# Sums of squares in the attention heads: exact fp32 products replaced by a rounded square and its remainder, and one temporary moved

## The chip, the cores and the metric

One Trainium2 chip, one of its cores. The metric is the device time of one execution in microseconds (us), lower is better. The kernel is a single launch. Its engines work from separate instruction streams and meet at semaphores: TensorE (PE, with its weight loads as PEld), VectorE (DVE), ScalarE (ACT), GpSimd (POOL) and SyncE (SP).

## What is computed

Two blocks run one after the other on a sequence of 1024 tokens with 1024 channels. The second has two layers over 1040 tokens (16 meta tokens in front, padded to 1044 columns here). The change is in its attention, 8 heads of 96 dimensions in each layer. The rest (pooling, gates, projections, the whole first block) is untouched. The part that matters:

```python
def rmsnorm_2(x, gain):
    xf = x.astype(jnp.float32)
    inv = lax.rsqrt(jnp.mean(xf * xf, axis=-1, keepdims=True) + NORM_EPS)
    return (xf * inv * gain.astype(jnp.float32)).astype(x.dtype)

def mla(...):
    q = (c_q @ w_q_b).reshape(B, L, N_HEADS, QK_HEAD_DIM)
    kv = (c_kv @ w_kv_b).reshape(B, L, N_HEADS, QK_NOPE_DIM + V_HEAD_DIM)
    k_nope, v = kv[..., :QK_NOPE_DIM], kv[..., QK_NOPE_DIM:]
    k_pe = jnp.broadcast_to(k_rope_raw[:, :, None, :], (B, L, N_HEADS, QK_ROPE_DIM))
    k = jnp.concatenate([k_nope, k_pe], axis=-1)
    q = rmsnorm_2(q, g_qn)
    k = rmsnorm_2(k, g_kn)
    # rotation of the last 32 dimensions of q and k, then causal softmax attention
```

So every head needs, for each token, the sum of 96 squares of its query and the sum of 96 squares of its key. Tokens lie along the free dimension and the 96 dimensions along partitions, so the sum runs over partitions and is made by TensorE: a product with a matrix of ones (`ones96`, with zeros in the 32 rows that hold the rolled copy for the rotation) leaves the sum in every row of a PSUM bank.

## The kernel before

**Precision.** Products that need fp32 accuracy are made of values split in two: `hi` is the value rounded to the fp32r type, `lo` the remainder, and hi*hi, hi*lo and lo*hi are added up in PSUM. The two sums of squares are the exception: `key_sum` (L985) and `query_sum` (L995) multiply plain fp32 squares by plain fp32 ones in one matmul instruction each. The profile shows such an instruction as two matmul records and two weight loads.

**A head.** For head g the 1044 columns are cut into three waves: two of 384 columns and one of 276. A wave goes: `key_value_part` (L957) leaves raw keys and values in the bank `acc_n`; ACT (`key_value_evict`, L1638 and two copies) squares the keys and moves keys and values out; `query_part` (L973, three parts of six matmuls) leaves raw queries in `acc_q`; ACT (`query_squares`, L1654) squares them. `key_sum` then fills `acc_n` again, ACT (`key_scale`, L1664 Ln and L1667 Exp) makes the inverse root, `turn_values` (L1006) transposes the values into the same `acc_n`, ACT copies them out (`values_in`, L1202), `query_sum` fills `acc_n` a third time and ACT (`query_scale`, L1675 and L1678) makes the queries' inverse root. Each user of `acc_n` waits for the reader before it. DVE applies the rotation to the queries (`query_table`, L2342 to L2344), scales and splits the keys (`key_norm`, L2364 to L2368) and the queries (`query_norm`, L2352 to L2356), and reduces rough scores to row maxima (`maximum`, L2377).

**The order of work** is written out by hand, with no planner. Every engine runs `for h in range(-1, MH)` and in it 15 steps `n`. In a pass h, PE makes the scores, the exponents' products with the values and the later rough scores of head h, and between them the waves of head g = h + 1, with wave 0 at n = 0 to 4, wave 1 at n = 5 to 9 and wave 2 at n = 10 to 14. The pass h = -1 has no scores: it only prepares head 0. The last pass prepares nothing. There are thus 16 heads prepared in all, 14 of them inside a pass that also has scores and 2 (one for each layer) in an opening pass. `key_sum` stands at n = 2, 7, 12, `turn_values` at n = 3, 8, 13 and `query_sum` at n = 4, 9, 14. PE's first matmul that needs a normalized wave is `rough_scores` (L1022): at n = 7 for wave 0 (it waits for `q_hi` and `k_hi`), at n = 12 for wave 1, at n = 2 of the next pass for wave 2.

DVE's stream is in order, and `do` makes it wait for the completion of each of its instructions. Its order in a pass is: n=0 `key_norm` of wave 2, n=1 `query_norm` of wave 2, n=2 two maxima, n=3 maximum, `head_out` (L2394, L2395) of the pass before, maximum, n=4 `query_table` of wave 0 and two maxima, n=5 a maximum, `maxima_of`, `key_norm` of wave 0, n=6 `head_out`, `query_norm` of wave 0, n=7 and n=8 a maximum each, n=9 maximum, `query_table` of wave 1, n=10 `key_norm`, n=11 `query_norm` of wave 1, n=12 two maxima, n=13 two maxima and `head_out`, n=14 maximum, `maxima_of`, `query_table` of wave 2. In the pass h = -1 DVE also makes constants at n = 6 and n = 8.

**Ahead of the heads** DVE splits eight chunks of the latent activations (L2326, by the helper at L1818 and L1819), each when PE has released the chunk. `ones96` is a slice of the constants; its rows for the rotated part of the keys find their squares in `X[:, 6, :]` (L1607, once for each layer).

**Memory.** The rotation's temporary `rope_tmp` (L214) lies in the work buffer `R_` behind the row maxima. `G_` is an fp32r view of rows 8 to 15 of that buffer.

**POOL** splits the streamed weights, one unit of 1024 columns for each head in this stage, and no part of it is in the change. SP only issues the loads of weights.

Of the kernel before, what the change touches and what calls it, by code (L numbers as in the profile page):

```python
# [7 lines left out]
F32 = mybir.dt.float32  # L8
F32R = mybir.dt.float32r
I32 = mybir.dt.int32  # L10
ALU = mybir.AluOpType
# [4 lines left out]
P = 128  # L16
# [132 lines left out]
def build(nc, xT, metaT, pos, params, consts, bands, lru_w, wstream, outT):  # L149
    with ExitStack() as ctx:  # L150
# [59 lines left out]
        ident_r, causal_r, after_r = (G_[:, idr0 + P * i:idr0 + P * i + P] for i in range(3))  # L210
        row_max = G_[:, idr0 + 3 * P:idr0 + 3 * P + 34 * TB]
        extra0 = idr0 + 3 * P + 34 * TB
        assert extra0 + QP <= 8 * RW
        rope_tmp = R_[:, 8 * RW + extra0:8 * RW + extra0 + QP]  # L214
        head_inv = tuple(R[:, 18, QP * i:QP * i + QP] for i in range(2))
        qb = tuple(X_[:, 4 * TP + QP * i:4 * TP + QP * i + QP] for i in range(2))
        qsq = tuple(X_[:, 4 * TP + QP * i:4 * TP + QP * i + QP] for i in (2, 3))
# [78 lines left out]
        for name in tuple(f"x_in{j}" for j in range(KC)) + tuple(f"reload{j}" for j in range(KC)) + (  # L296
            "consts_in", "meta_in", "lru_in", "bands_in", "xre_in",
            "w_in0", "w_in1", "w_hi_done", "w_lo_done", "unit_done",
            "ready0", "ready1", "free0", "free1",
            "aux_ready0", "aux_ready1", "aux_free0", "aux_free1",  # L300
            "a_ready", "a_used",
            "f_ready",
            "sq_ready", "sq_free", "sum_ready", "rs_ready", "x_squared", "x_paired",
            "dve_step", "act_step",
            "to_dve", "to_act", "to_pe",
            "act_to_pe",
            "spilled", "m_spilled", "g_spilled", "g_spilled_late", "stored", "pos_in", "t_spilled", "t_in",
            "kv_raw", "q_raw", "k_free", "q_free", "k_squared", "q_squared", "k_sum", "q_sum", "kn_free", "qn_free",
            "rs_k", "rs_q", "k_normed", "q_normed", "k_hi", "q_hi", "k_lo", "q_lo",
            "v_turned", "v_in",  # L310
            "rough_ready", "rough_max", "max_ready", "max_turned", "max_row",
            "s_ready", "p_in",
            "piece_done", "piece_free", "piece_squared", "piece_total", "piece_summed", "piece_scale",
            "piece_y", "piece_hi", "piece_lo",
            "lru_done", "conv_done", "conv_summed", "conv_centred", "conv_squared", "conv_variance", "conv_rs",
            "conv_normed", "gate0", "gate1", "gate_log", "conv_gate", "vt_ready", "vt_copied", "sc_ready", "sc_free", "sc_max", "sc_exp", "mx_ready", "max_taken",
            "pt_ready", "pt_copied", "av_ready", "av_copied", "sum_taken", "weights_due", "weights_ready",
            "gain_squared", "gain_root", "meta_squared", "meta_summed", "meta_scale", "weighed", "plain",
            "weighed_free", "plain_free", "x1_squared", "x1_total", "x1_summed", "x1_scale", "x1_done",
            "pv_done", "pv_ready0", "pv_ready1", "inv_ready", "inv_used", "av_free0", "av_free1",  # L320
        ):
            sems[name] = sem(name)
# [129 lines left out]
        def _(pe):  # L452
# [435 lines left out]
            for l in range(LAYERS):  # L888
# [90 lines left out]
                def key_sum(g, pc):  # L979

                    k = wave(l, g, pc)
                    c0, w = QP * pc, piece_width(pc)
                    pe.wait_ge(*n_free[0])
                    pe.wait_ge(sems["k_squared"], k)
                    nc.tensor.matmul(acc_n[:, 0:w], ones96, X[:, 6, c0:c0 + w], start=True,  # L985
                                     stop=True).then_inc(sems["k_sum"], 1)
                    n_free[0] = (sems["kn_free"], k)

                def query_sum(g, pc):

                    k = wave(l, g, pc)
                    w = piece_width(pc)
                    pe.wait_ge(*n_free[0])
                    pe.wait_ge(sems["q_squared"], k)
                    nc.tensor.matmul(acc_n[:, 0:w], ones96, qsq[k % 2][:, 0:w], start=True,  # L995
                                     stop=True).then_inc(sems["q_sum"], 1)
                    n_free[0] = (sems["qn_free"], k)

                def turn_values(g, pc):
# [98 lines left out]
                for h in range(-1, MH):  # L1098
                    g = h + 1
                    more = g < MH  # L1100
                    for n in range(NB):
# [6 lines left out]
                        if more:  # L1108
                            if n in (7, 8, 9):
                                rough_scores(g, n - 7, 0)  # L1110
                            if n == 12:
                                rough_scores(g, 3, 0)
                            if n == 13:
                                rough_scores(g, 4, 1)
                            if n == 14:
                                rough_scores(g, 5, 1)
                            if n in (0, 5, 10):
                                key_value_part(g, n // 5)
                            if n % 5 in (1, 2, 3):
                                query_part(g, n // 5, n % 5 - 1)  # L1120
                            if n in (2, 7, 12):
                                key_sum(g, n // 5)
                            if n in (3, 8, 13):
                                turn_values(g, n // 5)
                            if n in (4, 9, 14):
                                query_sum(g, n // 5)
                            if n == 10:
                                turn_maxima(g, 0)
                            if n in (12, 13):
                                rough_scores(g, n - 8, 0)  # L1130
# [43 lines left out]
        def _(act):  # L1174
# [364 lines left out]
            for l in range(LAYERS):  # L1539
# [93 lines left out]
                def key_value_evict(g, pc):  # L1633
# [1 line left out]
                    k = wave(l, g, pc)  # L1635
                    c0, w = QP * pc, piece_width(pc)
                    act.wait_ge(sems["kv_raw"], k)
                    do(nc.scalar.activation(X[top, 6, c0:c0 + w], acc_n[top, 0:w], ACT.Square), "k_squared")  # L1638
                    if k > 2:
                        act.wait_ge(sems["k_lo"], k - 2)  # L1640
                    do(copy(kb[k % 2][top, 0:w], acc_n[top, 0:w], param(f"kn_{l}", 0, top)))
# [2 lines left out]
                def query_squares(g, pc):  # L1644
# [6 lines left out]
                        await_unit(0)  # L1651
                    if k > 2:
                        act.wait_ge(sems["q_normed"], k - 2)
                    do(nc.scalar.activation(qsq[k % 2][:, 0:w], acc_q[:, 0:w], ACT.Square), "q_squared")  # L1654

                def key_scale(g, pc):

# [126 lines left out]
        def _(dve):  # L1784
# [423 lines left out]
            for l in range(LAYERS):  # L2208
# [110 lines left out]
                for j in (6, 7, 0, 1, 2, 3, 4, 5):  # L2319
# [3 lines left out]
                    else:  # L2323
                        c["a_used"].step()
                        dve.wait_ge(sems["a_used"], c["a_used"].value())
                    split(R[:, 8 + j, wide], Ah[:, j, :], Al[:, j, :], "a_ready")  # L2326
                await_free(0)
                await_free(1)
                do(vec.tensor_copy(S_[:, 40:41], S_[:, 60:61]), "to_act")
                top = slice(64, 128)  # L2330

                def query_table(g, pc):
# [1 line left out]
                    k = wave(l, g, pc)  # L2334
                    c0, w = QP * pc, piece_width(pc)
                    q = qb[k % 2]
                    if pc == NQP - 1:
                        unit.step()
                    dve.wait_ge(sems["q_squared"], k)
                    if k > 2:  # L2340
                        dve.wait_ge(sems["q_lo"], k - 2)
                    do(vec.tensor_tensor(q[:, 0:w], acc_q[:, 0:w], R[:, 17, c0:c0 + w], ALU.mult), "q_free")  # L2342
                    do(vec.tensor_copy(rope_tmp[rope, 0:w], q[ROPE:2 * ROPE, 0:w]))
                    do(vec.tensor_tensor(q[rope, 0:w], q[rope, 0:w], rope_tmp[rope, 0:w], ALU.add))  # L2344

                def query_norm(g, pc):

# [66 lines left out]
                for h in range(-1, MH):  # L2414
# [4 lines left out]
                    for n in range(NB):  # L2419
                        if h >= 0:  # L2420
                            if n == 0:
                                key_norm(h, 2)
                            if n == 1:
                                query_norm(h, 2)
                        if more and n == 4:
                            query_table(g, 0)
                        if h >= 0:
# [221 lines left out]
```

## Time and profile before

| what | value |
|---|---|
| median of 3 runs | 3119.41 us (3118.04 to 3122.75) |
| the profiled execution, its own time | 3116.02 us |
| its span | 3113.5 us (2.5 us of its time lie outside the span) |
| mean granted TensorE clock | 0.991 |
| PE busy | 2999.5 us, 96% of the span |
| DVE busy | 1426.5 us, 46% |
| ACT busy | 738.6 us, 24% |
| POOL busy | 1109.3 us, 36% |
| chain that ended last, PE's share | 89%; DVE 8%; ACT 2% |

The page gives busy shares of the whole span. The chain that ended last follows each instruction back to what released it, and lists the pieces with their start and length; in it a matmul stands with the time by which it moved the end of the matmuls on, while the timeline shows each matmul from its own start to its own end, and these overlap. "issue" in the chain is time in which the engine waited for nothing that the profile could name. The heads of the two layers are at about 1688 to 2012 us and 2644 to 2967 us, and their passes repeat every 38.8 us.

### The profile page before, as it was taken

How to read it: one execution, taken by the hardware profiler on the slowest of the kernel's cores; microseconds unless marked ns; L12 is line 12 of the kernel's file. 1: busy time of each engine (PE TensorE's matmuls, PEld its weight loads, DVE VectorE, ACT ScalarE, POOL GpSimd, SP SyncE). 2: the span in 40 equal slices, each digit the busy share in tenths (PEclk: the TensorE clock that was granted, in tenths of full speed). 3: DMA queues.
4: the chain of work that ended last, by engine and by line, in shares of the span. 5: the costliest groups of instructions: out<-in, count | busy, mean ns of one | idle time of the engine just before them, and what ended most of it. 6: DMA issues, size and time to landing. Idle time of an engine off the chain costs nothing.

```text
span 3113.5 us, 41248 instructions
## 1 busy us (share of the span) xinstructions
PE 2999.5 (96%) x16332; PEld 2672.7 (86%) x16332; DVE 1426.5 (46%) x1781; ACT 738.6 (24%) x1285; POOL 1109.3 (36%) x1335
## 2 busy tenths in 40 slices
PE   7999889999999999899999999999999999899999
PEld 5777667888888888899998888899999999788899
DVE  3796754332222349500114666656520022666761
ACT  3144421000000023001112555402100111555500
POOL 3652144444444445433433111143533433111132
PEclk9999999999999999999999999999999999999999
DMA  2111111111111111212112000241312112000142
GB/s 112 48 34 38 70 52 42 48 47 47 47 47 47 47 48 69 76 44 101 48 62 75 15 15 14 79 142 41 112 53 96 48 49 89 27 15 15 38 169 81
DMA packets 47444, 182.60 MB, mean 59 GB/s; under 512 B 6080, under 2 KB 6208, under 8 KB 46912
## 3 DMA queue, kind: packets, MB, share of 16 engines
q1 hardware_dynamic: 31248, 113.19, 10.9%
q10 hardware_dynamic: 16048, 67.28, 5.7%
q8 instruction: 113, 1.85, 0.2%
q14 instruction: 35, 0.29, 0.0%
HBM read 150.06 MB, written 30.39 MB: 58 GB/s over the span
## 4 chain that ended last, share of the span: by engine, by line
PE 89%; DVE 8%; ACT 2%; issue 1%; DMA 0%; POOL 0%; ACTq 0%; DVEq 0%; POOLq 0%
PE acc L476 66%; PE acc L973 4%; PE aux L1089 4%; PE acc L1068 4%; PE acc L581 3%; PE acc L1022 2%; PE acc L957 1%; PE acc L985 1%; PE acc L995 1%; DVE act_lo L1851 1%; DVE work L1858 1%; DVE act_lo L1819 1%; PE acc L1006 0%; DVE work L2232 0%; DVE residual L2248 0%
## 5 line engine op out<-in xcount | busy, mean ns | idle before, releaser
L404 POOL TENSOR_TENSOR w_lo<-w_raw,w_hi 128x256 fp32r<-128x256 f32 (+1 forms) x924 | 849.0, 949 | 17.2
L476 PE MATMUL acc<-act_hi,w_hi 128*128 128x348 f32 (+1 forms) x2896 | 709.6, 345 | 31.0 <-DVE work L2257 8.3
L476 PE MATMUL acc<-act_lo,w_hi 128*128 128x348 f32 (+1 forms) x2896 | 707.9, 344 | 0.0
L476 PEld LDWEIGHTS acc<-act_hi,w_hi 128*128 128x128 f32 x2896 | 506.0, 189 | 76.0 <-issue 30.3
L476 PE MATMUL acc<-act_hi,w_lo 128*128 128x348 f32 (+1 forms) x2896 | 562.1, 344 | 0.0
L476 PEld LDWEIGHTS acc<-act_lo,w_hi 128*128 128x128 f32 x2896 | 507.6, 189 | 39.3
L424 POOL TENSOR_TENSOR small<-shape_consts 128x1 f32<-128x1 f32 x192 | 45.4, 236 | 1367.1 <-PE acc L476 1257.4
L476 PEld LDWEIGHTS acc<-act_hi,w_lo 128*128 128x128 f32 x2896 | 490.5, 188 | 39.4
L476 PE MATMUL acc<-ff_split,w_hi 128*128 128x512 f32 (+1 forms) x1376 | 314.0, 375 | 3.2 <-DVE ff_split L1819 3.2
L476 PEld LDWEIGHTS acc<-ff_split,w_hi 128*128 128x128 f32 x1376 | 246.9, 188 | 50.1 <-DVE ff_split L1819 4.3
L2107 DVE TENSOR_TENSOR residual<-acc,residual 128x1024 f32<-128x1024 f32 (+1 forms) x82 | 100.7, 1228 | 383.1 <-PE acc L476 383.0
L413 POOL CAST w_hi<-w_raw 128x1024 fp32r<-128x1024 f32 x23 | 25.6, 1115 | 596.3 <-PE acc L973 510.1
L1068 PE MATMUL acc<-ff_split 128*128 128x276 f32 (+5 forms) x864 | 208.6, 354 | 0.1
L425 POOL CAST w_hi<-w_raw 128x1024 fp32r<-128x1024 f32 x192 | 201.5, 1050 | 0.0
L1089 PE MATMUL aux<-work 128*128 128x276 f32 (+5 forms) x576 | 175.4, 400 | 0.0
L1483 ACT ACTIVATE work<-acc 128x1024 f32<-128x1024 f32 x32 | 32.7, 1026 | 574.3 <-PE acc L476 568.0
L1068 PEld LDWEIGHTS acc<-ff_split 128*128 128x128 f32 x864 | 140.8, 190 | 31.3 <-issue 0.7
L476 PE MATMUL acc<-ff_split,w_lo 128*128 128x512 f32 (+1 forms) x688 | 166.6, 373 | 0.0
L1707 ACT ACTIVATE work<-acc 128x384 f32<-128x384 f32 (+2 forms) x240 | 104.4, 435 | 200.5 <-PE acc L1068 149.8
L2156 DVE TENSOR_TENSOR work<-work 128x1024 f32<-128x1024 f32 x32 | 40.7, 1273 | 239.9 <-ACT work L1483 239.8
L1202 ACT ACTIVATE work<-acc 64x384 f32<-64x384 f32 (+5 forms) x153 | 93.4, 620 | 217.4 <-PE acc L476 177.2
L476 PEld LDWEIGHTS acc<-ff_split,w_lo 128*128 128x128 f32 x688 | 124.2, 188 | 22.0
(296 smaller groups left out, 3765.0 us busy)
## 6 DMA issues: line engine op xcount, KB each, us to landing
w_raw<-in_wstream SPq DMA_DIRECT2D x215, 512.0 KB, 3.2
spill_m<-residual ACTq DMA_DIRECT2D x2, 4176.0 KB, 13.1
spill_g<-work ACTq DMA_DIRECT2D x16, 522.0 KB, 2.7
residual<-spill_m ACTq DMA_DIRECT2D x16, 522.0 KB, 5.9
work<-spill_g ACTq DMA_DIRECT2D x16, 522.0 KB, 8.2
residual<-spill_x ACTq DMA_DIRECT2D x16, 522.0 KB, 4.1
spill_x<-residual ACTq DMA_DIRECT2D x8, 522.0 KB, 4.5
spill_x<-residual ACTq DMA_DIRECT2D x1, 4176.0 KB, 11.6
```

Of the source, the lines that this page charges most:

```text
L404: ins = nc.gpsimd.tensor_tensor(Wl[:, s, c0:c0 + w], Wraw[:, s, c0:c0 + w], Wh[:, s, c0:c0 + w].bitcast(F32), ALU.subtract)
L424: nc.gpsimd.tensor_tensor(S_[:, 62:63], C_[:, 128:129], C_[:, 128:129], ALU.add)
L425: nc.gpsimd.tensor_copy(Wh[:, s, :], Wraw[:, s, :]).then_inc(sems["w_hi_done"], 1)
L476: ins = nc.tensor.matmul(acc[0:m, s, p, 0:w], wt[:, ws, w0 + j * m:w0 + j * m + m], x[:, k, p * w:p * w + w], start=(first and t == 0), st ...
L581: ins = nc.tensor.matmul(acc[:, s, p, 0:w], wt[:, ws, k * P:k * P + P], x[:, k, p * w:p * w + w], start=(first and t == 0), stop=(end and ...
L973: ins = nc.tensor.matmul(acc_q[:, 0:w], wt[:, w_head[0], j * P:j * P + P], x[:, j, c0:c0 + w], start=(j == 0 and t == 0), stop=(j == 5 and ...
L1022: ins = nc.tensor.matmul(acc_r[bank][:, 0:n], qh[:, min(P * i, LASTQ):min(P * i, LASTQ) + P], kh[:, 512 * p:512 * p + n], start=True, stop ...
L1068: ins = nc.tensor.matmul(out, k2[kt][:, c0:c0 + P], q2[qt][:, lo:lo + w], start=m == 0, stop=(m == 2 and not diag))
L1089: ins = nc.tensor.matmul(aux[:, b % 2, lo - QP * pc:lo - QP * pc + w], values(h)[:, t, :], prob(k)[:, at:at + w], start=t == 0, stop=end)
L1202: return nc.scalar.activation(out, in_, ACT.Copy, scale=scale)
L1707: do(nc.scalar.activation(prob(k)[:, 0:w], src, ACT.Exp), "p_in")
L2107: do(vec.tensor_tensor(x, acc_view(s, pieces), x, ALU.add), f"free{s}")
```

## The change

Four things, all in the attention stage:

- The squares are kept twice. ACT squares each wave a second time, with output in the fp32r type (`k_sq[0]`, `q_sq[0]`), beside the fp32 squares. DVE then subtracts the rounded square from the exact one (`key_square_low` at n = 1, 6, 11 and `query_square_low` at n = 4, 9, 14, both ahead of the other work of their step), which gives `k_sq[1]` and `q_sq[1]`. The rows of the rotated keys are split once for each layer after chunk 7 of the eight chunks.
- `key_sum` and `query_sum` are two fp32r matmuls each (high part, then remainder) against `ones96_r`, an fp32r copy of the ones that DVE makes once for each layer. They wait for the remainder, not for the square.
- In the pass h = -1, `key_sum` goes to n = 3, 8, 13, right ahead of `turn_values`; in the other passes it stays.
- `rope_tmp` moves from the work buffer into chunk 6 of the residual buffer. `query_table` no longer waits for `q_squared`; that wait is in `query_square_low`.

```diff
-        rope_tmp = R_[:, 8 * RW + extra0:8 * RW + extra0 + QP]
+        q_sq = tuple(G_[:, extra0 + QP * i:extra0 + QP * i + QP] for i in range(2))
+        ones96_r = G_[:, extra0 + 2 * QP:extra0 + 2 * QP + P]
+        k_sq = tuple(G_[:, 6 * RW + TP * i:6 * RW + TP * i + TP] for i in range(2))
+        rope_tmp = X_[:, 6 * TP + QP:6 * TP + 2 * QP]
...
 def key_sum(g, pc):
-                    pe.wait_ge(sems["k_squared"], k)
-                    nc.tensor.matmul(acc_n[:, 0:w], ones96, X[:, 6, c0:c0 + w], start=True,
-                                     stop=True).then_inc(sems["k_sum"], 1)
+                    pe.wait_ge(sems["k_square_low"], k)
+                    for i in range(2):
+                        ins = nc.tensor.matmul(acc_n[:, 0:w], ones96_r, k_sq[i][:, c0:c0 + w], start=(i == 0), stop=(i == 1))
+                    ins.then_inc(sems["k_sum"], 1)
...
 def query_sum(g, pc):
-                    pe.wait_ge(sems["q_squared"], k)
-                    nc.tensor.matmul(acc_n[:, 0:w], ones96, qsq[k % 2][:, 0:w], start=True,
-                                     stop=True).then_inc(sems["q_sum"], 1)
+                    pe.wait_ge(sems["q_square_low"], k)
+                    for i in range(2):
+                        ins = nc.tensor.matmul(acc_n[:, 0:w], ones96_r, q_sq[i][:, 0:w], start=(i == 0), stop=(i == 1))
+                    ins.then_inc(sems["q_sum"], 1)
...
-                            if n in (2, 7, 12):
+                            if n in ((3, 8, 13) if h < 0 else (2, 7, 12)):
                                 key_sum(g, n // 5)
...
 def key_value_evict(g, pc):
-                    do(nc.scalar.activation(X[top, 6, c0:c0 + w], acc_n[top, 0:w], ACT.Square), "k_squared")
+                    if k > 1:
+                        act.wait_ge(sems["k_square_low"], k - 1)
+                    nc.scalar.activation(X[top, 6, 0:w], acc_n[top, 0:w], ACT.Square)
+                    do(nc.scalar.activation(k_sq[0][top, c0:c0 + w], acc_n[top, 0:w], ACT.Square), "k_squared")
...
 def query_squares(g, pc):
-                    do(nc.scalar.activation(qsq[k % 2][:, 0:w], acc_q[:, 0:w], ACT.Square), "q_squared")
+                    nc.scalar.activation(qsq[k % 2][:, 0:w], acc_q[:, 0:w], ACT.Square)
+                    do(nc.scalar.activation(q_sq[0][:, 0:w], acc_q[:, 0:w], ACT.Square), "q_squared")
...
                     split(R[:, 8 + j, wide], Ah[:, j, :], Al[:, j, :], "a_ready")
+                    if j == 7:
+                        split(X[rr, 6, :], k_sq[0][rr, :], k_sq[1][rr, :], "dve_step")
                 await_free(0)
                 await_free(1)
+                do(vec.tensor_copy(ones96_r, ones96))
...
 def query_table(g, pc):
-                    if pc == NQP - 1:
-                        unit.step()
-                    dve.wait_ge(sems["q_squared"], k)
...
+                def key_square_low(g, pc):
+                    dve.wait_ge(sems["k_squared"], k)
+                    do(vec.tensor_tensor(k_sq[1][top, own], X[top, 6, 0:w], k_sq[0][top, own].bitcast(F32),
+                                         ALU.subtract), "k_square_low")
+
+                def query_square_low(g, pc):
+                    if pc == NQP - 1:
+                        unit.step()
+                    dve.wait_ge(sems["q_squared"], k)
+                    do(vec.tensor_tensor(q_sq[1][:, 0:w], qsq[k % 2][:, 0:w], q_sq[0][:, 0:w].bitcast(F32),
+                                         ALU.subtract), "q_square_low")
...
+                        if more and n in (1, 6, 11):
+                            key_square_low(g, n // 5)
+                        if more and n in (4, 9, 14):
+                            query_square_low(g, n // 5)
                         if more and n == 4:
                             query_table(g, 0)
```

## Rows read from the trace of the kernel before

**Rows 1.** The page's first part: busy time, share of the span, instructions of each engine.

```profile
PE 2999.5 (96%) x16332; PEld 2672.7 (86%) x16332; DVE 1426.5 (46%) x1781; ACT 738.6 (24%) x1285; POOL 1109.3 (36%) x1335
```

**Rows 2.** Stretches: us, busy of PE, PEld, DVE, ACT, POOL, clock, DMA.

```profile
1690.50:1709.00 18.50, 15.35 (x73) 11.97 (x72) 14.69 (x29) 9.05 (x20) 5.18 (x5) 0.91 0.19 61
...
1857.00:1896.00 39.00, 38.38 (x229) 33.31 (x228) 26.31 (x54) 23.05 (x52) 5.06 (x9) 1.00 0.05 14
```

**Rows 3.** Chain that ended last, one steady pass: start us, us, what.

```profile
1840.00 1.04 PE acc L973 x6
1841.04 0.65 PE acc L985 x2
...
1854.00 0.16 issue
...
1863.86 0.76 PE acc L973 x6
...
1865.47 0.46 issue
...
1867.27 0.47 PE acc L985 x2
```

**Rows 4.** Timeline of PE, query_sum of three waves: start us, us, instruction.

```profile
1833.28 0.68 PE L995 MATMUL acc<-residual,shape_consts 128*128 128x276 f32 x2
...
1846.56 0.81 PE L995 MATMUL acc<-residual,shape_consts 128*128 128x384 f32 x2
...
1860.23 0.86 PE L995 MATMUL acc<-residual,shape_consts 128*128 128x384 f32 x2
```

**Rows 5.** Timeline of DVE in steady passes; in brackets its idle time before.

```profile
1832.01 0.69 DVE L2377 TENSOR_REDUCE small<-acc 128x1 f32<-128x512 f32 x1 [1.28 <-PE acc L1022]
...
1833.32 0.55 DVE L2395 TENSOR_TENSOR residual<-aux,residual 64x384 f32<-64x384 f32 x1
1833.90 0.42 DVE L2377 TENSOR_REDUCE small<-acc 128x1 f32<-128x256 f32 x1
...
1838.88 0.45 DVE L2356 TENSOR_TENSOR ff_split<-residual,ff_split 128x276 fp32r<-128x276 f32 x1
...
1845.36 0.69 DVE L2377 TENSOR_REDUCE small<-acc 128x1 f32<-128x512 f32 x1 [0.24 <-PE acc L1026]
1846.08 0.56 DVE L2342 TENSOR_TENSOR residual<-acc,work 128x384 f32<-128x384 f32 x1
...
1853.69 0.36 DVE L2355 CAST ff_split<-residual 128x384 fp32r<-128x384 f32 x1
...
1865.47 0.36 DVE L2355 CAST ff_split<-residual 128x384 fp32r<-128x384 f32 x1
```

**Rows 6.** Timeline of ACT, wave 1 of a steady pass.

```profile
1857.79 0.58 ACT L1664 ACTIVATE residual<-acc,small 128x384 f32<-128x384 f32 x1
1858.40 0.52 ACT L1667 ACTIVATE residual<-residual 128x384 f32<-128x384 f32 x1
1858.83 0.47 ACT L1654 ACTIVATE residual<-acc 128x384 f32<-128x384 f32 x1
1859.20 0.32 ACT L1202 ACTIVATE work<-acc 128x192 f32<-128x192 f32 x1
```

**Rows 7.** Chain that ended last, opening passes of both layers.

```profile
1697.72 2.19 PE acc L957 x6
...
2648.37 1.67 DVE act_lo L1819
2650.08 0.80 PE acc L973 x3
...
2651.60 0.57 DVE residual L2342
...
2657.26 0.33 PE acc L1022
```

**Rows 8.** Timeline of DVE ahead of the heads.

```profile
1675.38 1.25 DVE L1819 TENSOR_TENSOR act_lo<-work,act_hi 128x1044 fp32r<-128x1044 f32 x1
1677.51 0.70 DVE L1818 CAST act_hi<-work 128x1044 fp32r<-128x1044 f32 x1 [0.88 <-PE acc L476]
```

More of the change, by code:

```diff
@@ L212, in build @@
         extra0 = idr0 + 3 * P + 34 * TB
-        assert extra0 + QP <= 8 * RW
-        rope_tmp = R_[:, 8 * RW + extra0:8 * RW + extra0 + QP]
+        q_sq = tuple(G_[:, extra0 + QP * i:extra0 + QP * i + QP] for i in range(2))
+        ones96_r = G_[:, extra0 + 2 * QP:extra0 + 2 * QP + P]
+        k_sq = tuple(G_[:, 6 * RW + TP * i:6 * RW + TP * i + TP] for i in range(2))
+        assert extra0 + 2 * QP + P <= 6 * RW and 2 * TP <= 2 * RW
+        rope_tmp = X_[:, 6 * TP + QP:6 * TP + 2 * QP]
         head_inv = tuple(R[:, 18, QP * i:QP * i + QP] for i in range(2))
@@ L307, in build @@
             "spilled", "m_spilled", "g_spilled", "g_spilled_late", "stored", "pos_in", "t_spilled", "t_in",
-            "kv_raw", "q_raw", "k_free", "q_free", "k_squared", "q_squared", "k_sum", "q_sum", "kn_free", "qn_free",
+            "kv_raw", "q_raw", "k_free", "q_free", "k_squared", "q_squared", "k_square_low", "q_square_low", "k_sum", "q_sum", "kn_free", "qn_free",
             "rs_k", "rs_q", "k_normed", "q_normed", "k_hi", "q_hi", "k_lo", "q_lo",
@@ L2344, in query_table @@
                     do(vec.tensor_tensor(q[rope, 0:w], q[rope, 0:w], rope_tmp[rope, 0:w], ALU.add))
+                def key_square_low(g, pc):
+                    k = wave(l, g, pc)
+                    c0, w = QP * pc, piece_width(pc)
+                    own = slice(c0, c0 + w)
+                    dve.wait_ge(sems["k_squared"], k)
+                    do(vec.tensor_tensor(k_sq[1][top, own], X[top, 6, 0:w], k_sq[0][top, own].bitcast(F32),
+                                         ALU.subtract), "k_square_low")
+                def query_square_low(g, pc):
+                    k = wave(l, g, pc)
+                    w = piece_width(pc)
+                    if pc == NQP - 1:
[3 more added lines that the diff above has]
+                                         ALU.subtract), "q_square_low")
                 def query_norm(g, pc):
```

## The prediction

> **What bounds the kernel now.** I read the page's busy shares first: PE is busy for 96% of the span, DVE for 46% [rows 1], so on the average only PE's time should count. The average is not what decides here, so I went to the stage that the change touches. In a steady pass of the heads PE is busy for 38.4 of 39 us at full clock and DVE for 26.3 [rows 2]. Then the chain that ended last, inside one pass: nearly all of it is PE, but it breaks twice, 0.16 us ahead of L1022 at 1854.15 us and 0.46 us ahead of L1022 at 1865.93 us, both named "issue" [rows 3]. The timeline of DVE says who it is: L2355, which writes the `q_hi` that L1022 waits for, ends at 1854.05 and at 1865.83 us [rows 5], 0.10 us before PE goes on each time. So twice in a pass PE already arrives a little ahead of DVE. From 1845.36 us, where a maximum was released by PE, to L2355 at 1853.69 [rows 5] the timeline marks no idle time of DVE. PE bounds the pass, with DVE's two runs right beside it.
>
> **What TensorE saves.** A sum of 384 fp32 columns moves the chain by 0.65 us, one of 276 by 0.47 us [rows 3]. Six fp32r matmuls of 384 columns take 1.04 us and six of 276 take 0.76 [rows 3], so two take 0.35 and 0.25. Saved: 0.30 us for each of four sums and 0.22 for each of two, 1.64 us for a head, 26.2 us for 16 heads. That is all that the change can give.
>
> **What it adds on DVE, steady passes.** The remainders are plain subtractions. One of 384 columns has L2342's price, 0.56 us and 0.03 to the next (0.59); one of 276 has that of L2356, 0.45 and 0.03 (0.48) [rows 5]. Six of them make 3.3 us for a head, and DVE would still be idle for a quarter of the pass. What counts is where they stand. I follow the pass by the points at which PE releases DVE and DVE releases PE.
>
> Wave 2, n = 14. `query_square_low` stands behind the maximum at 1832.01 (released by PE) and the two `head_out` steps of n = 13. The last of these ends at 1833.87 and the next instruction begins at 1833.90 [rows 5]. The remainder takes that slot: 1833.90 + 0.45 + 0.10 to PE = 1834.45. PE wants its `query_sum` at 1833.28 [rows 4]. It waits 1.17 us, and behind it in PE's stream are a product with values and all of the next head's scores.
>
> Wave 0, n = 4 to 7. DVE's run from 1845.36 to `q_hi` gets two subtractions more: the query's remainder (n = 4) and the key's of wave 1 (n = 6). `q_hi` is 1.18 us later, and L1022, already the waiting one, starts 1.18 us later. On the way PE waits also for the remainder itself (1846.08 + 0.56 + 0.10 = 1846.74 against 1846.56 [rows 4]), but that and what `query_sum` saves both lie inside the stretch that now ends with DVE, and count for nothing.
>
> Wave 1, n = 9 to 12. ACT squares at 1858.83 and would go on at 1859.20 [rows 6]; a second square there ends at 1859.67. With 0.10 to DVE (as from DVE to PE), 0.56 and 0.10 the sum starts at 1860.43 against 1860.23 [rows 4]. This lies again in a stretch that ends with DVE: the maximum that opens it is released by PE before the sum. DVE's run to L2355 at 1865.47 gets the key's remainder of wave 2, 0.48 us, and L1022 comes 0.48 later.
>
> Savings that stay are those of sums outside these stretches: `key_sum` of the three waves, 0.30 + 0.30 + 0.22, and `query_sum` of wave 2, 0.22, together 1.04. A steady pass: 1.17 + 1.18 + 0.48 - 1.04 = **+1.79 us**, in 14 passes **+25.1 us**.
>
> **The two opening passes (h = -1).** No scores cover anything here, the work is a chain through PE, ACT and DVE. Before, PE's last product ends at 2650.88 us and DVE's `query_table` starts at 2651.60 [rows 7]. After: DVE ends its splits at 2650.04 [rows 7], copies the ones (below 0.3) and makes the key's remainder (0.59), so that `key_sum`, moved to n = 3, starts at about 2651.2 and ends 0.35 later; 0.25 to ACT (an estimate: PE's sum at 1860.23 plus 0.65 in the chain ends at 1860.88, and ACT's reader comes about 0.25 behind such a sum); then Ln 0.61, Exp 0.43, square 0.37 from start to start, the second square 0.47 [rows 6], 0.10 to DVE, the remainder 0.59. `query_table` starts at 2654.4, 2.8 us late, and the key's remainder of wave 1 makes `q_hi` 3.4 us late at L1022 (2657.26 [rows 7]). For wave 1 the constants on DVE cover most of the longer chain; at least its two subtractions remain (0.59 + 0.48), at most the 2.8 and 0.48; I take 1.6, near the lower end, since DVE has work there. For wave 2, between 0.5 and 2.3, I take 1.0, for the sum that has now to follow the maximum of n = 13. That makes 6.0 us a layer. In the first layer the clock is at half there already [rows 2, 7], and I add 1.0 for products on the longer chain. Together **+13 us**, between 8 and 20.
>
> **What costs nothing.** ACT's second squares (some 2.4 us a head) fall in a pass in which it is busy for 23 of 39 us [rows 2]; where one does lie on the path, it is counted above. If that cover went, a maximum's row or an exponent would come up to 0.5 us late. The split of the rotated keys' squares, 0.70 + 1.25, lies behind a chunk after which DVE is idle for 0.88 us, and again after the next ones [rows 8]: hidden, at most 2 us a layer. The moved temporary has the same shapes and partitions, and no other queue is passed by anything. No DMA is added.
>
> **The sum.** +25.1 + 13 = +38.1 us on the profiled execution's 3116.0, that is 3154.1; it stands 3.4 us below the median, so against the median of 3119.4 I forecast **3157 us**.
>
> **The rivals.**
> *The clock falls in the steady passes.* Two more waits of over 1 us and one of half that come into each pass. In the opening pass of the first layer, where PE is busy for 15.35 of 18.50 us, the granted clock is 0.91 on the average [rows 2], which is 3.3 us (2 x 0.09 x 18.5) at 1.2 GHz instead of 2.4, and six products take 2.19 us instead of about 1.1 [rows 7]. One such fall in each pass loses 1.7 us of products, of which waits swallow up to half: +12 to +24 us more, 3169 to 3181. Against it: a pass with these waits is still some 90% busy, and the waits stand 12 us and more apart. Chance 0.10. The Trainium skill ("TensorE: Matmul & The Clock Gate", Part 1: The HAM clock gate) has it that the slow clock is the default and that activity releases it; it speaks for this rival, and the opening passes agree with it, while no row of before shows it between dense passes.
> *Faster: the remainders fall in idle time, and PE's saving comes through.* Its place is L1022 at n = 7 and n = 12. The profile names "issue" there and not DVE, and DVE has 12.7 idle us in a pass. If PE did not in fact wait for DVE there, and DVE caught up within its gaps, 14 passes would give 23 us and the openings take 13: 3119 - 23 + 13 = 3109. It decides where the new waits of a pass together stay under 0.7 us, since 14 x (1.64 - 0.7) is the openings' 13. Against it: L2355 ends 0.10 us before PE goes on at both places, and the 1.17 us at n = 14 need no assumption on either. Chance 0.08.
> *The waits overlap.* If the wait at n = 14 alone were absorbed, the pass costs 0.62 us and the whole comes to +22, 3141. Chance 0.12, and another 0.04 that this goes so far that nothing can be measured (within 0.2%, 6.2 us, about what a measurement of this kernel can tell from no change).
> *It doesn't do what it says:* the rounded products run at the price of the exact ones, two for one. Then the four sums outside DVE's stretches cost 0.95, 0.95, 0.69 and 0.69 more than I have, 3.3 us in a pass and 46 in 14: 3203. L973's rows are of the same type and take about a quarter per column [rows 3], so 0.02.
>
> **How the numbers follow.** The forecast, DVE's runs setting the pace, has 0.64. Its own range comes from the steady passes (0.9 to 2.6 us each, according to whether one wait is absorbed or a second square delays another step) and the openings (8 to 20): 3140 to 3176. That takes in most of the overlap rival and half of the clock's, and leaves out about 0.2. Faster by over 0.2%: 0.08. Within: 0.04. Slower: 0.88.
>
> **What would show it.** PE's matmul records stay 16332 in number, DVE's instructions rise by about 102 and ACT's by 96. The sums' rows fall to 0.35 and 0.25 in the chain. Steady passes repeat after 40.6 us instead of 38.8. Waits ahead of L995 (n = 14, 1.2 us, by DVE's subtraction) and of L1022 at n = 7 (1.1 to 1.3 us) and n = 12 (0.9) appear; a pass that repeats after 37.2 us would prove me wrong, as would L1022 waiting at n = 7 no longer than before. The openings grow by 6 to 7 us each. A granted clock below 0.98 in steady passes would mean the clock's rival. Everything outside the heads keeps its times.

## The result, and the profile after

| what | before | after |
|---|---|---|
| median | 3118.72 us (4 runs, 3115.37 to 3122.75) | 3169.82 us (4 runs, 3169.14 to 3172.13) |
| the profiled execution, its own time | 3116.02 us | 3172.13 us |
| its span | 3113.5 us | 3170.3 us |
| mean granted TensorE clock | 0.991 | 0.982 |
| one steady pass (wave 0's transposition to the next head's) | 38.79 us | 40.65 us |

The ratio is 1.0164, 95% interval 1.0151 to 1.0176: 51 us slower. The forecast was 3157 us, 38 slower, in a range of 3140 to 3176. The two profiled executions lie 56 us apart because one stands 2.7 us below its median and the other 2.3 above; 5.3 us of that arises ahead of the heads, where nothing was changed (the memset ahead of the activations' splits starts at 1665.91 us before and at 1671.22 after).

The page's first part, after, against [rows 1]:

```profile
PE 3006.7 (95%) x16332; PEld 2685.0 (85%) x16332; DVE 1482.7 (47%) x1883; ACT 772.3 (24%) x1381; POOL 1110.0 (35%) x1335
```

PE has as many matmuls as before, and is busy for 7 us more, not 26 less: the sums are shorter, but more products ran at half clock. How much of the difference that is was not worked out. DVE has the 102 instructions more that were forecast, ACT the 96. The stretches, against [rows 2] (us, busy of PE, PEld, DVE, ACT, POOL, granted clock, DMA): a steady pass and the openings of both layers.

```profile
1796.00:1837.00 41.00, 37.50 (x226) 32.72 (x225) 29.77 (x61) 25.16 (x58) 5.02 (x9) 1.00 0.04 14
...
1699.00:1737.00 38.00, 25.60 (x97) 21.95 (x98) 24.47 (x51) 13.64 (x32) 6.98 (x12) 0.69 0.05 17
2681.00:2719.00 38.00, 25.47 (x106) 21.53 (x107) 26.04 (x56) 14.51 (x34) 6.90 (x11) 0.70 0.08 28
```

PE is busy for 37.5 of 41 us in a pass, where it was 38.4 of 39. In the openings the clock is at 0.69 and 0.70: most of the time TensorE ran at 1.2 GHz. Before, the clock is at 0.91 and 0.96 in stretches as long at the same place (1694 to 1732 us and 2649 to 2687).

The chain that ended last, parts of one steady pass after, against [rows 3]:

```profile
1796.03 0.91 issue
1796.94 0.30 PE acc L1027
...
1798.44 0.35 PE acc L989 x2
...
1803.00 0.59 PE acc L1000 x2
...
1807.97 0.93 issue
1808.89 0.47 PE acc L1027
...
1810.24 0.26 PE acc L989 x2
...
1813.58 0.70 DVE small L2405
1814.30 0.85 DVE residual L2422
1815.17 0.56 DVE residual L2423
1815.76 0.46 DVE pool_split L2371
1816.22 0.14 issue
1816.35 0.50 PE acc L1000 x2
```

L989 is `key_sum`, L1000 `query_sum`, L1027 the rough scores (before: L985, L995, L1022). A key's sum of 384 columns costs 0.35 us and one of 276 0.26, as forecast. The waits ahead of L1027 have grown from 0.16 to 0.91 and from 0.46 to 0.93. At n = 14 the chain leaves PE altogether and goes through DVE: a maximum, the two steps of `head_out` (L2422, L2423), the remainder (L2371), and only then the sum. That is the wait of the forecast's first step, in the order in which it gave it. (This pass took 40.95 us: the first step of `head_out`, L2422, lasted 0.85 in it, where it lasts 0.56 in the passes of 40.65.)

The two places at which PE waits ahead of its rough scores cut a pass into three stretches. Before, from `turn_values` of wave 0 to L1022 at n = 7, to L1022 at n = 12, to the next head's `turn_values`:

```profile
1844.43 0.33 PE acc L1006 x3
1854.15 0.30 PE acc L1022
1865.93 0.47 PE acc L1022
1883.23 0.33 PE acc L1006 x3
```

The same places after, in a pass of 40.65:

```profile
1827.00 0.33 PE acc L1011 x3
1837.89 0.30 PE acc L1027
1849.85 0.47 PE acc L1027
1867.64 0.33 PE acc L1011 x3
```

The three stretches have grown from 9.72 to 10.89, from 11.78 to 11.96 and from 17.30 to 17.79 us: by 1.17, 0.18 and 0.49.

### The profile page after: what moved, and what is told of

It reads as the page before. It is cut to its first block, busy times and chain, and to the rows that moved or that the text cites. A ratio compares the mean times of both kernels' runs of the same rounds, so it can differ in the third digit from the quotient of the medians.

```text
span 3170.3 us, 41586 instructions
## 1 busy us (share of the span) xinstructions
PE 3006.7 (95%) x16332; PEld 2685.0 (85%) x16332; DVE 1482.7 (47%) x1883; ACT 772.3 (24%) x1381; POOL 1110.0 (35%) x1335
## 4 chain that ended last, share of the span: by engine, by line
PE 86%; DVE 9%; issue 2%; ACT 2%; DMA 0%; POOL 0%; ACTq 0%; DVEq 0%; POOLq 0%
PE acc L479 65%; PE acc L976 4%; PE aux L1094 4%; PE acc L1073 3%; PE acc L584 2%; PE acc L960 2%; PE acc L1027 2%; DVE small L2405 1%; PE acc L1000 1%; DVE act_lo L1860 1%; DVE work L1867 1%; DVE pool_split L2371 1%; DVE act_lo L1828 1%; PE acc L989 1%; PE acc L1011 0%
```

## The experiments

Times are medians; a pass is read from each profiled execution as in the table above.

| run | time, us | ratio to before (95%) | steady pass, us |
|---|---|---|---|
| after | 3169.8 | 1.0151 to 1.0176 | 40.65 |
| e1, exact opening | 3146.8 | 1.0070 to 1.0104 | 40.65 |
| e2, query's remainder early | 3154.3 | 1.0096 to 1.0130 | 39.67 |
| e3, keys' remainders late | 3151.7 | 1.0085 to 1.0119 | 39.60 |
| e4, no remainders | 3101.1 | 0.9921 to 0.9954 | 37.15 |
| e5, products that fill the opening | 3166.0 | 1.0128 to 1.0162 | 40.66 |
| e6, before, only key_sum moved | 3121.7 | 0.9996 to 1.0015 | 38.79 |
| e7, before, head_out late | 3111.4 | 0.9967 to 0.9990 | 38.39 |
| e8, all moves | 3109.2 | 0.9954 to 0.9982 | 38.06 |
| e9, e8 with three orders changed | 3103.2 | 0.9941 to 0.9966 | 37.52 |
| e10, e9's orders, exact sums | 3106.2 | 0.9953 to 0.9979 | 37.90 |
| e11, e1 to e3 together | 3117.7 | 0.9991 to 1.0008 | 38.62 |

**e1: what do the openings cost?** Only head 0 of each layer goes back to exact sums, the old order and its old temporary.

```diff
 def key_sum(g, pc):
+    if g == 0:
+        pe.wait_ge(sems["k_squared"], k)
+        nc.tensor.matmul(acc_n[:, 0:w], ones96, X[:, 6, c0:c0 + w], start=True,
+                         stop=True).then_inc(sems["k_sum"], 1)
+        n_free[0] = (sems["kn_free"], k)
+        return
...
-                            if n in ((3, 8, 13) if h < 0 else (2, 7, 12)):
+                            if n in (2, 7, 12):
```

> The changed kernel, but the opening passes (head 0 of each layer) use the exact fp32 sums in the old order; the 14 steady passes stay changed. By the prediction's term the openings cost 6.5 us each, so this is about 13 us below the changed kernel's 3170 (3157). By the trace of the changed kernel, whose heads take 25 us more in each layer while a steady pass repeats after 40.6 to 41.0 us, they cost 11 to 12.5 each, and this comes at 3145 to 3148, with the granted clock back at 0.99. If the openings were innocent it would stay at 3170.

Measured: 3146.8 us, 23.0 below the changed kernel, with the steady pass unchanged at 40.65. So the two openings cost 11.5 us each, against 6.5 in the forecast (in the profiled executions, from the memset to head 1's `turn_values`, the changed kernel takes 12.0 and 10.9 us more than the one before), and the steady passes have the rest: 14 x 1.86 = 26.0 of the 28 us that e1 still lies above the kernel before. One pass of its profile stands at 42.2 instead of 40.65: the clock fell in it.

**e2: the wait at n = 14.**

```diff
-                        if more and n in (4, 9, 14):
+                        if more and n in (4, 9):
                             query_square_low(g, n // 5)
...
                             if n == 13:
                                 maximum(g, 4, 1)
+                                query_square_low(g, 2)
                                 maximum(g, 5, 0)
```

> The changed kernel with one move: the query's remainder of wave 2 goes from behind head_out (n = 14) to ahead of the maximum of rough scores 5 at n = 13. If the wait of 1.2 us at that sum is a full loss in every pass, 14 x 1.1 = 15 to 17 us come back (3153 to 3155), and a pass repeats after 39.5 us. If DVE's later run then becomes late by the same, nothing comes back (3170).

Measured: 3154.3 us, 15.5 back, and a pass of 39.67, 0.98 less. L1000 at 276 columns now starts with no idle time ahead of it; in the changed kernel the same line of PE's timeline carries a wait. The columns are start us, us, engine, instruction, and in brackets the idle time before it.

The changed kernel:

```profile
1856.98 0.49 PE L1000 MATMUL acc<-pool_split 128*128 128x276 f32 x2 [1.06 <-DVE pool_split L2371]
```

e2:

```profile
1849.70 0.47 PE L1000 MATMUL acc<-pool_split 128*128 128x276 f32 x2
```

The rival of the expectation, that DVE's later run becomes late instead, came in with a small part. In the chain the sum starts 1.04 us sooner behind the product ahead of it and takes 0.31 instead of 0.49, together 1.22. But L1027 at n = 2 of the next pass, which takes 0.23 in the changed kernel, takes 0.47 in e2:

```profile
1863.29 0.23 PE acc L1027
```

```profile
1855.98 0.47 PE acc L1027
```

In e2 DVE's cast for it (L2383) ends at 1855.87, 0.10 us before it, which is the distance at the other waits for DVE: PE is now just held up there. 1.22 less 0.24 is the 0.98 of the pass.

**e3: the subtractions ahead of L1027.**

```diff
-                        if more and n in (1, 6, 11):
+                        if more and n in (1, 7, 12):
                             key_square_low(g, n // 5)
```

> The changed kernel with the keys' remainders of waves 1 and 2 moved from ahead of query_norm (n = 6, 11) to behind it (n = 7, 12). If the two runs of DVE that end in L1022's operand set the pace, 14 x (0.59 + 0.48) = 15 us come back (3155), and the waits ahead of L1022 fall from 0.91 to about 0.3 and from 0.93 to 0.45 us. If the waits that the profile names issue have another cause, it stays at 3170, or gets slower since the key's sum now waits.

Measured: 3151.7 us, 18.1 back, and a pass of 39.60, 1.05 less, where 0.59 + 0.48 = 1.07 was expected. That makes 14.7 us in 14 passes. In the profiled execution the openings are 5.4 us shorter as well, since the move holds there too; three more passes with a fall of the clock (see below) take 4.7 us of it back. The chain of e3 in one pass:

```profile
1873.14 0.32 issue
...
1884.48 0.46 issue
```

The two waits are 0.32 and 0.46 us, where they were 0.91 and 0.93. What the profile calls "issue" there is DVE. This run's profile has five passes of 41.2 to 41.5 us, and its clock is 0.981, below the changed kernel's 0.982, although it waits less in the pass.

**e4: no remainders at all.** Each sum is one product of the rounded squares; what is left out is the remainder, so the sums are less exact.

```diff
-                    pe.wait_ge(sems["k_square_low"], k)
-                    for i in range(2):
-                        ins = nc.tensor.matmul(acc_n[:, 0:w], ones96_r, k_sq[i][:, c0:c0 + w], start=(i == 0), stop=(i == 1))
+                    pe.wait_ge(sems["k_squared"], k)
+                    pe.wait_ge(sems["k_square_low"], l + 1)
+                    ins = nc.tensor.matmul(acc_n[:, 0:w], ones96_r, k_sq[0][:, c0:c0 + w], start=True, stop=True)
...
```

The query's sum is cut down in the same way, and the second squares on ACT and the subtractions on DVE are gone.

> The changed kernel with the remainders left out: each sum is one fp32r product of the rounded squares, so the sums are less exact; no subtraction on DVE, one square on ACT. If DVE's subtractions are the whole cost of the steady passes, they fall to about 37.2 us (sums outside DVE's stretches save 0.48 + 0.48 + 0.34 + 0.34), 23 us below the kernel before in 14 passes; the openings keep the moved key sum and part of their longer chain, 5 to 10 us: 3100 to 3108. If something else that came with the change (the moved temporary, the fp32r output of ACT) costs the time, it stays above 3130.

Measured: 3101.1 us, a pass of 37.15, where 37.2 was worked out from the waits. The moved temporary, ACT's fp32r output and the moved key sum are all still in this kernel, and it is 18 us faster than the one before. They are not what costs; the subtractions on DVE, with ACT's second square and the second product, are, as a group; e4 does not part them.

**e5: is it the clock in the openings?** 48 extra products a layer are placed where TensorE waits; their results are not used.

```diff
+                def filler(count):
...
+                    for _ in range(count):
+                        nc.tensor.matmul(aux[:, 0, 0:QP], Ah[:, 6, 0:P], Ah[:, 7, 0:QP], start=True, stop=True)
...
+                        if h < 0:
+                            filler({3: 5, 4: 8, 5: 3, 7: 12, 9: 6, 10: 3, 12: 3, 14: 8}.get(n, 0))
```

> The changed kernel with extra products in the two opening passes only (48 for a layer, of 384 columns, into a bank that is free there), placed where TensorE waits anyway; their result is not used. They can only take time in those places, unless they keep the clock up. If TensorE's half clock (1.2 GHz) explains what the openings cost beyond the forecast's chain (11 to 12.5 us instead of 6.5), 8 to 12 us come back (3158 to 3162) and the granted clock of the openings rises. If the openings cost what they do by a chain longer than forecast, it stays at 3170 or gets up to 5 us slower.

Measured: 3166.0 us, 3.8 back, less than half of what the first theory said, and not the 0 of the second. The stretches of e5:

```profile
1699.00:1737.00 38.00, 31.86 (x158) 28.22 (x157) 24.08 (x55) 16.02 (x38) 5.29 (x11) 0.82 0.08 28
2681.00:2719.00 38.00, 31.90 (x171) 28.50 (x170) 25.78 (x57) 16.94 (x39) 5.33 (x10) 0.91 0.08 28
```

The clock rose from 0.69 to 0.82 and from 0.70 to 0.91, so it did not become full, and the filler itself came onto the path in both layers, in its longest rows at half clock:

```profile
1702.09 2.86 PE aux L1107 x8
...
2683.83 2.64 PE aux L1107 x8
```

So the 3.8 us (the intervals of e5 and of the changed kernel overlap a little) are not the price of the half clock but what is left after the filler's own time. The second layer's stretches of e5 part the two, from L1027 at n = 7 to the one at n = 12 and on to head 1's `turn_values`:

```profile
2692.66 0.33 PE acc L1027
...
2704.36 0.63 PE acc L1027
...
2721.77 0.33 PE acc L1011 x3
```

The first takes 11.70 us in e5, 13.10 in the changed kernel and 10.12 before; the second 17.41, 18.12 and 16.36. With the clock up, these two cost 1.6 and 1.05 us more than before, where the forecast had 1.6 and 1.0 (the second with 1.40 us of filler on its path). From the memset to L1027 at n = 7, where the filler lies on the path, e5 takes 41.23 against 41.91: next to nothing came back. The Trainium skill has the slow clock as the default that activity releases ("TensorE: Matmul & The Clock Gate", Part 1: The HAM clock gate). The openings agree: extra products alone raised their clock.

**e6: the moved key sum alone**, in the kernel before.

```diff
-                            if n in (2, 7, 12):
+                            if n in ((3, 8, 13) if h < 0 else (2, 7, 12)):
                                 key_sum(g, n // 5)
```

> The kernel before, with only the order of the opening passes changed (the key's sum at n = 3, 8, 13). If the exposed wait for the key's Ln matters by itself, each opening grows by 1 to 3 us: 3121 to 3125. If the move is free, 3119.

Measured: 3121.7 against 3120.2 us for the kernel before in the same comparison; the interval holds 1. A cost of up to 0.15% is not excluded, a gain of more than 0.04% is. In the profiled executions its openings take 2.0 and 2.6 us longer than those before, so some of e1's 23 us may be the moved sum's; the times do not show it.

**e7: `head_out` of wave 0 behind `query_norm`**, in the kernel before.

```diff
-                            if n == 6:
+                            if n == 6 and not more:
                                 head_out(h, 0)
...
+                            if n == 7 and h >= 0:
+                                head_out(h, 0)
```

> The kernel before, with head_out of wave 0 moved behind query_norm (n = 6 to n = 7). DVE's run to L1022 gets 1.17 us shorter, but TensorE waited there for only 0.16 us: 14 x 0.16 = 2 us at most (3117). A control for the next kernel: if it gains much more, the order and not the cheaper sums is what pays there.

Measured: 3111.4 us against 3120.2, and a pass of 38.39, 0.40 less and not 0.16. This expectation missed, and its chain says why. L1022 at n = 7, before at 1854.15 with 0.30 us of its own behind the wait of 0.16, stands in e7 with no wait and 0.06:

```profile
1887.38 0.06 PE acc L1022
```

A wait costs PE's chain its own length and, here, 0.24 us on the first product behind it. Fourteen times 0.40 is 5.6 of the 8.8 us; the interval (3.1 to 10.3 us) holds both, and the steady passes show no more.

**e8: all moves together**: the edits of e1, e2, e3 and e7 in the changed kernel, so split sums in the steady passes and exact ones in the openings.

> Split sums in the steady passes with exact ones in the openings, the query's remainder of wave 2 early, the keys' remainders of waves 1 and 2 behind query_norm, head_out of wave 0 behind query_norm. By the theory that only the placement of the six subtractions costs, TensorE's saving comes through in all places but the sum of wave 1, about 1.3 us a pass: 3119 - 18 = 3101, between 3096 and 3106, a pass repeats after 37.4 us. If DVE's work as such costs (its amount, not its place), it stays above the kernel before.

Measured: 3109.2 us, a pass of 38.06: faster than before, but 8 us short of what was expected. Its chain shows a release by DVE that neither the forecast nor this expectation had counted, ahead of the 20 columns of rough score 8 (here L1044) at n = 5, which wait for the maximum (L2439) of the same bank:

```profile
1850.96 0.70 DVE small L2439
1851.66 0.04 issue
1851.70 0.28 PE acc L1044
...
1867.93 0.46 issue
```

**e9 and e10: the order mended, with split and with exact sums.** In e9 that maximum goes ahead of the rotation (`query_table` makes its first step there, `query_turn` the other two behind the maxima), the rotation of wave 1 goes ahead of a maximum, and ACT squares before its Exp. e10 has the same orders and the sums of the kernel before.

```diff
+                            if more and n == 4:
+                                query_table(g, 0)
...
                                 maxima_of(2)
+                                if more:
+                                    query_turn(g, 0)
...
+                            if n == 9 and h >= 0:
+                                query_table(g, 1)
                             if n in (7, 8, 9):
                                 maximum(g, n - 7, 0)
```

> e8 with three orders changed for the waits that its trace still shows (0.65 us ahead of the small rough score 8 at n = 5, which waits for a maximum, and 0.46 us ahead of L1022's place at n = 12): the maximum of rough score 8 goes ahead of the query's rotation, whose last two steps follow the maxima, the rotation of wave 1 goes ahead of a maximum, and ACT squares before its Exp. If these waits are all that stands between the pass of 38.05 us and TensorE's own time, a pass takes 37.0 us and the kernel 3109 - 14 = 3095. If other waits take their place, it stays at 3109.

> The same orders with the sums of the kernel before (exact fp32, no remainders). If the split sums are worth their price once they are placed well, this is slower than e9 by what TensorE saves, 14 x 1.64 = 23 us less what e9 leaves: 3105 to 3112 against 3095. If the order alone brings the gain, both are the same.

Measured: 3103.2 us for e9, the fastest kernel with full sums here, 15 us below the kernel before (3118.1 in that comparison), and 3106.2 for e10. e9 missed its expectation of 3095 and a pass of 37.0: it has 37.52. The waits left in e9's pass, with the first product behind each:

```profile
1862.33 0.32 issue
1862.65 0.47 PE acc L1044
...
1881.71 0.07 issue
1881.78 0.59 PE acc L1017 x2
```

Two more rows of that pass are longer with no wait shown ahead of them, a sum with 0.52 where 0.35 was forecast and a rough score with 0.44 where e10 has 0.23:

```profile
1857.42 0.52 PE acc L1017 x2
...
1874.88 0.44 PE acc L1044
```

With e10 the chain of a pass has no "issue" at all, and it takes 37.90 us. TensorE's saving would bring that to 37.90 - 1.64 = 36.26; e9 has 37.52, so three quarters of the saving, 1.26 us, are lost again. The rows give the most of it: 0.32 + 0.24 and 0.07 + 0.24 for the two waits, 0.17 and 0.21 for these two rows, together 1.25. The medians are 3 us apart. The intervals of the ratios to the kernel before overlap, but all six runs of e9 (3099.84 to 3105.08) lie below all six of e10 (3105.80 to 3110.90), and 14 x 0.38 = 5.3 us was to be expected from the pass. So most of e9's gain comes from the order, and the split sums add 3 to 5 us.

**e11: the three costs together**: the edits of e1, e2 and e3 in the changed kernel, in their old order otherwise.

> The changed kernel with the exact openings, the early query remainder and the late key remainders together (e1, e2 and e3 in one). If the three costs add up, 3170 - 23 - 15.5 - 18 = 3113, 6 us below the kernel before, and a pass takes 38.6 us. If they overlap, it is slower than 3119.

Measured: 3117.7 us against 3118.1 before, a pass of 38.62 as worked out (40.65 less 0.98 and 1.05). The three undoings alone gave 23.0, 15.5 and 18.1 us, in sum 56.6; together they give 52.1. So they account for the whole 51 us by which the change is slower, with an overlap of a few us: e2 and e3 also shorten the openings, by 1.5 and 5.4 us in the profiled executions, and e1 undoes these anyway. The expectation's 3113 had not taken that off.

## Why the prediction was right, point by point

- **TensorE's saving** was sized rightly: 0.35 and 0.26 us for the sums, against 0.35 and 0.25. Only the sums that start behind a wait cost more, 0.59 and 0.50 instead of 0.35 and 0.25, for the 0.24 us that e7 showed. The forecast did not know of it.
- **The three stretches of a pass** were forecast at +1.18, +0.18 (0.48 less a sum's saving of 0.30) and +0.43 (1.17 less 0.22, 0.22 and 0.30); they are +1.17, +0.18 and +0.49. So that the pass came out right is not luck: each part of it did.
- **The wait at n = 14** was forecast at 1.17 us. The chain has 1.04, and with the dearer product behind it 1.22, of which e2 got 0.98 back.
- **The subtractions in DVE's two runs** were forecast at 0.59 and 0.48 (keys) and 0.59 (query, wave 0). e3 took out 1.05 for the first two. The steady pass as a whole was forecast 1.79 us longer and is 1.86: +26.0 us in 14 passes, against +25.1. The reading that "issue" ahead of L1022 meant DVE, because DVE's result ended 0.10 us before, held.
- **One release was overlooked**: the small rough score at n = 5 waits for a maximum behind the remainder. In the changed kernel it cost nothing of its own, since it lies in the stretch that ends with DVE at n = 7 anyway (the wait there is 0.91 us, not the 1.1 to 1.3 forecast, as PE has been held up earlier). It did cost in e8, once that stretch was mended.
- **The openings are the term that was mis-sized**: 6.0 us a layer and 1.0 for the clock, 13 in all; e1 measured 23.0. The first wave is seen in the rows of the second layer, after, against [rows 7]:

```profile
2682.06 0.65 DVE pool_split L2340
...
2682.92 0.80 DVE pool_split L2361
...
2683.86 0.99 PE acc L989 x2
...
2687.58 0.99 PE acc L1000 x2
...
2689.23 2.30 PE acc L960 x6
...
2695.05 0.33 PE acc L1027
```

  The copy of the ones took 0.65 us and not below 0.3, the first remainder 0.80 and not 0.59, the two sums 0.99 each and not 0.35, and the six products of the next wave 2.30 instead of 1.15, so that DVE then waited for the keys' squares. From the memset (2621.46 us before, 2653.14 after) to this L1027 it is 35.80 us before and 41.91 after: +6.1 instead of +3.4. The later waves of the same opening end in these rows, before and after:

```profile
2667.38 0.76 PE acc L1022
...
2683.74 0.33 PE acc L1006 x3
```

```profile
2708.15 0.48 PE acc L1027
...
2726.27 0.33 PE acc L1011 x3
```

  That is +3.0 where the forecast had 1.6, and +1.8 where it had 1.0. In the first layer the three are +5.8, +3.2 and +3.1. For wave 1 the forecast let the constants on DVE cover most of the longer chain. They ended at 1717.53 us in the first layer, and the remainder began there at 1719.50, 1.96 us later, on ACT's square: that cover was too short there.

  By these rows the larger part of what is missing in the second layer is the clock, for which the forecast put 1.0 in the first layer and nothing in the second. Of the second layer's 4.9 us above its 6.0, e5 gave 1.4 and 0.7 back in the two later stretches. In the stretch up to L1027 it is an estimate: a sum behind a wait takes 0.60 at full clock (the first layer's first one, at 1701.94) and six such products 1.28 (e5), against 0.99 twice and 2.30, in all 1.8 us. That makes 3.9 of the 4.9. The rest are the ones, the remainder and the 0.24 us behind each wait. No run has the openings at full clock with no filler on the path, so for the first stretch, and for the first layer, this is not shown.
- **The rival of the clock** came in, but in another place than it was put. It had a fall in every steady pass; the profile of the changed kernel has two of its passes at 42.2 us and the others near 40.65. In the openings the clock is at 0.7, where the forecast had it only as it was before, and with 1 us in one layer. The other rivals are out: e2 shows that four fifths of the wait at n = 14 were not absorbed, e3 that PE does wait for DVE ahead of L1027, and the rounded products cost what L973's rows said.
- **The exactness of the total**: of the 51 us measured, 25.1 + 13 were forecast; 0.9 are missing in the passes, 10 in the openings, and some 2 are left; the two steady passes in which the clock fell are 3.1 us longer in the profiled execution.

## What to carry to other kernels

An engine that is busy for 96% of the span can still be paced by one that is busy for 46% of it: look in the chain for the places at which the bound engine already waits, even for 0.2 us, and price added work by whether it stands in the run of instructions that ends there. Here six subtractions of 0.5 us in each of 14 passes made the steady passes 26 us longer in one order of VectorE's stream, TensorE's saving already taken off, and cost less than they save in another. And work that gains where another stage covers it can lose in the pass that has no cover; in e1 the old form was kept there, and that alone brought 23 us back.

## What was not expected of the hardware

A wait of TensorE costs more than its length: the first product behind it moves the chain by 0.24 us more than it does without the wait (0.30 against 0.06, 0.47 against 0.23 for 512 columns, 0.59 against 0.35 for the two products of a sum of 384 columns), and by a little less in two other places (0.28 against 0.06 for 20 columns, 0.49 against 0.31 for a sum of 276). Taking away a wait of 0.16 us made the pass 0.40 us shorter (e7), and e2 lost 0.24 us again where PE came to be held up with no wait shown in the chain.

The clock fell to 1.2 GHz also inside steady passes in which TensorE is busy for more than nine tenths, in two passes of the changed kernel, two of e5, one of e1 and five of e3, each then 1.5 to 1.9 us longer, and in none of the kernel before or of e2. e3 waits less than the changed kernel and had more such falls, so the length of the waits alone does not decide it; what does was not tried.

A cast of 128 x 128 from the constants took 0.64 us on VectorE at 1700.14 us, and the same shape takes 0.23 later in the same opening, at 1710.80. What slowed the first was not tried either.
